# Rotary halves swapped by GpSimd's SBUF-to-SBUF transfers in place of permutation products, the sign in the sine table

## What is computed

```python
def rope(t):
    ...
    t1, t2 = tf[..., : hd // 2], tf[..., hd // 2 :]
    rot = jnp.concatenate([-t2, t1], axis=-1)
    return (tf * jnp.cos(ang) + rot * jnp.sin(ang)).astype(t.dtype)
```

```python
def partial_rope(x, cos, sin):
    half = cos.shape[-1]
    rot = 2 * half
    xr = x[..., :rot].astype(jnp.float32)
    x1, x2 = xr[..., :half], xr[..., half:]
    out = jnp.concatenate([x1 * cos - x2 * sin, x2 * cos + x1 * sin], axis=-1).astype(x.dtype)
    return jnp.concatenate([out, x[..., rot:]], axis=-1)
```

## Time and profile before

| | |
|---|---|
| median of 3 runs | 3019.54 us (3014.81 to 3020.39) |
| span of the profiled execution | 3020.7 us |
| TensorE busy | 2978.3 us, 99% |
| VectorE busy | 2178.2 us, 72% |
| ScalarE busy | 1275.6 us, 42% |
| GpSimd busy | 128.6 us, 4% |
| mean granted clock of TensorE | 0.995 |
| projection 0 | about 489 to 635 us |
| projection 1 | about 1469 to 1617 us |
| projection 2 | about 2418 to 2566 us |

### The profile page before, as it was taken

The page is one execution under the profiler, slowest core; times in us unless marked ns, Lnnn a source line. Parts: engine busy times, 40 slices in busy tenths (PEclk is TensorE's granted clock), DMA queues, the critical chain, the costliest instruction groups (busy, mean ns, idle before and its releaser), DMA issues.

```text
span 3020.7 us, 46546 instructions
## 1 busy us (share of the span) xinstructions
PE 2978.3 (99%) x17415; PEld 2601.4 (86%) x17415; DVE 2178.2 (72%) x3215; ACT 1275.6 (42%) x1903; POOL 128.6 (4%) x121
## 2 busy tenths in 40 slices
PE   8999999999999999999999999999999999999998
PEld 7888888887888889998877899988998878799987
DVE  7577765765777678785688787867775478788753
ACT  4333223465332245452345554425454244654442
POOL 0000000000000000000031000000000013000000
PEclk9999999999999999999999999999999999999999
DMA  4355553213555533343322133442333322123332
GB/s 162 99 191 194 188 196 99 84 43 95 176 181 192 191 106 103 104 148 114 92 81 63 57 105 103 155 153 84 106 108 103 101 79 84 36 91 104 105 105 76
DMA packets 263452, 351.94 MB, mean 117 GB/s; under 512 B 16770, under 2 KB 208500, under 8 KB 263312
## 3 DMA queue, kind: packets, MB, share of 16 engines
q1 hardware_dynamic: 241344, 270.57, 28.8%
q0 software_dynamic: 21488, 79.09, 8.0%
q10 hardware_dynamic: 480, 0.35, 0.0%
HBM read 348.76 MB, written 2.10 MB: 116 GB/s over the span
## 4 chain that ended last, share of the span: by engine, by line
PE 87%; DVE 9%; ACT 2%; issue 2%; DMA 0%; POOL 0%; DVEq 0%; SPq 0%; ACTq 0%
PE bank L2237 18%; PE bank L2239 18%; PE bank L2238 18%; PE bank L2378 9%; PE bank L2380 9%; PE bank L2381 9%; DVE w_lo L1324 1%; PE bank L2298 1%; PE bank L2260 1%; PE bank L2263 1%; PE bank L2261 1%; DVE a_score L1824 1%; ACT w_hi L754 0%; DVE h_f L1379 0%; DVE h_lo L1385 0%
## 5 line engine op out<-in xcount | busy, mean ns | idle before, releaser
L1324 DVE TENSOR_TENSOR w_lo<-raw,w_hi 128x1024 fp32r<-128x1024 f32 x322 | 393.8, 1224 | 510.8 <-ACT w_hi L754 508.0
L754 ACT ACTIVATE w_hi<-raw 128x1024 fp32r<-128x1024 f32 x348 | 368.6, 1059 | 894.9 <-PE bank L2239 844.8
L2237 PE MATMUL bank<-h_hi,w_hi 128*128 128x512 f32 x1376 | 541.8, 394 | 4.3 <-POOL w_lo L702 2.6
L2239 PE MATMUL bank<-h_hi,w_lo 128*128 128x512 f32 x1376 | 537.1, 390 | 0.0
L2238 PE MATMUL bank<-h_lo,w_hi 128*128 128x512 f32 x1376 | 536.5, 390 | 0.0
L2237 PE MATMUL bank<-act_hi,w_hi 128*128 (+1 forms) x1120 | 437.8, 391 | 0.0
L2239 PE MATMUL bank<-act_hi,w_lo 128*128 (+1 forms) x1120 | 436.1, 389 | 0.0
L2238 PE MATMUL bank<-act_lo,w_hi 128*128 (+1 forms) x1120 | 435.8, 389 | 0.0
L2237 PEld LDWEIGHTS bank<-h_hi,w_hi 128*128 128x128 f32 x1376 | 259.0, 188 | 61.5 <-issue 8.1
L2239 PEld LDWEIGHTS bank<-h_hi,w_lo 128*128 128x128 f32 x1376 | 258.8, 188 | 54.8
L2238 PEld LDWEIGHTS bank<-h_lo,w_hi 128*128 128x128 f32 x1376 | 259.2, 188 | 52.5
(11 more groups left out here) (382 smaller groups left out, 5695.3 us busy)
## 6 DMA issues: line engine op xcount, KB each, us to landing
raw<-in_ffn_w_in_dram SPq DMA_DIRECT2D x176, 512.0 KB, 3.5
ada_w<-in_ada_w_dram POOLq DMA_DIRECT2D x72, 1024.0 KB, 5.6
raw<-in_ffn_w_out_dram SPq DMA_DIRECT2D x88, 512.0 KB, 3.6
raw<-in_ffn_w_gate_dram SPq DMA_DIRECT2D x44, 512.0 KB, 3.8
raw<-in_ffn_w_up_dram SPq DMA_DIRECT2D x44, 512.0 KB, 3.9
raw<-in_ffn_w_down_dram SPq DMA_DIRECT2D x44, 512.0 KB, 4.3
raw<-in_mix_w_in_dram SPq DMA_DIRECT2D x44, 512.0 KB, 3.6
raw<-in_attn_w_qkv_dram SPq DMA_DIRECT2D x24, 512.0 KB, 3.7
```

Of the source, the lines that this page charges most:

```text
L754: nc.scalar.activation(w_hi[:, nb % SPL, :], raw_slab(nb), ACT.Copy).then_inc(s_hi, 1)
L1324: V.tensor_tensor(w_lo[:, nb % SPL, :], raw_slab(nb), w_hi[:, nb % SPL, :].bitcast(F32), ALU.subtract).then_inc(s_lo, 1)
L2237: T.matmul(dst, wh, mh, start=first, stop=False)
L2239: return T.matmul(dst, wl, mh, start=False, stop=last)
```

## The change

The halves are now swapped by transfers. ScalarE's copy goes to st in plain float32; GpSimd issues, for each rotated tile, four transfers that write the rows of st with the halves of each head exchanged into swap (`swap_halves`): 32 rows of 2 KB each in projection 0, 8 rows each in projections 1 and 2. Each waits for the copy of its tile, and from tile 2 on for the rotation of the tile two before. VectorE waits for the four (`s_swap`, one semaphore for each place), multiplies swap by the sines in place and adds it to rot; st_lo, turned and the two products of a tile are gone. The sign now stands in the tables: in the sine table of projection 0, and for projections 1 and 2 in the frequencies of the first half (negative angle; the cosine is the same). The rows of swap that no transfer writes in projections 1 and 2 are cleared once per layer. The sums by quarters, which VectorE made at the start, come as a constant, and `keep_warm` reads a tile of ones. TensorE's counts for the transposed tiles (`s_postmm`) are renumbered, and these use bank 4 + idx % 2.

On GpSimd, in the order of its list, the place is projection 1: the tables' loads are followed by w_lo of slabs 10 to 22 before (the ISA row is the instruction that configures GpSimd for its subtraction; ada_w is the load of the next FFN).

The diff, cut:

```diff
-    half_turn = np.zeros((P, P), np.float32)
-    part_turn = np.zeros((P, P), np.float32)
...
+    quarters = np.tile(np.eye(32, dtype=np.float32), (4, 4))
...
+    sign = np.where(np.arange(P) % HD < HD // 2, -1.0, 1.0)[:, None]
+    rope = np.concatenate([np.cos(ang), sign * np.sin(ang)], 1).astype(np.float32)
...
-        small[h:h + rot // 2, 64] = f2
+        small[h:h + rot // 2, 64] = -f2
...
+        def swap_count(m, i):
+            return 64 * (((0, 8, 14), (0, 8, 13))[i % 2][m] + i // 2 + 1)
...
+            def swap_halves(m, i):
+                rows = HD // 2 if m == 0 else HD // 8
+                pool.wait_ge(s_actT, AT0[f"proj{m}"] + i + 1)
+                if i >= 2:
+                    pool.wait_ge(s_rot, RO0[m] + i - 1)
+                for h in (0, HD):
+                    for to, src in ((h, h + rows), (h + rows, h)):
+                        pool.dma_start(side["swap"][to:to + rows, i % 2, :], side["st"][src:src + rows, i % 2, :]).then_inc(s_swap[i % 2], 16)
...
             mix_tables(0)
+            for i in range(16):
+                swap_halves(0, i)
...
             mix_tables(1)
-            project_lo(1)
+            for i in range(9):
+                swap_halves(1, i)
+            project_lo(1, (POOL_LO[0], POOL_LO[0] + 3))
+            for i in (9, 10):
+                swap_halves(1, i)
+            project_lo(1, (POOL_LO[0] + 3, POOL_LO[1]))
...
-                            nc.scalar.activation(bufs["st_hi"][:, staged % 2, :], src, ACT.Copy).then_inc(s_actT, 1)
+                            nc.scalar.activation(bufs["st"][:, staged % 2, :], src, ACT.Copy).then_inc(s_actT, 1)
...
+                if step == 4:
+                    link(V.memset(side["swap"][:], 0.0))
...
-                        dve.wait_ge(s_postmm, PO0[m] + j + 1)
-                        if i:
-                            dve.wait_ge(s_rot, RO0[m] + i)
-                        link(V.tensor_tensor(bufs["turned"][:], aux[:], bufs["cos"][:, 1, :], ALU.mult))
-                        V.tensor_tensor(rot, rot, bufs["turned"][:], ALU.add).then_inc(s_rot, 1)
+                        swap = bufs["swap"][:, i % 2, :]
+                        dve.wait_ge(s_swap[i % 2], swap_count(m, i))
+                        link(V.tensor_tensor(swap, swap, bufs["cos"][:, 1, :], ALU.mult))
+                        V.tensor_tensor(rot, rot, swap, ALU.add).then_inc(s_rot, 1)
...
-                        V.tensor_tensor(bufs["st_lo"][:, j % 2, :], src, bufs["st_hi"][:, j % 2, :].bitcast(F32), ALU.subtract)
...
-            V.tensor_copy(turn_hi[:], squares[:, 1:3, :]).then_inc(s_ones, 1)
...
-                            T.matmul(aux[:], turn, bufs["st_hi"][:, j % 2, :], start=True, stop=False)
-                            pe.wait_ge(s_dveT2, RO0[m] + rotated[0] + 1)
-                            ins = T.matmul(aux[:], turn, bufs["st_lo"][:, j % 2, :], start=False, stop=True)
```

90 lines of the change are left out of this document (41 added, 49 removed).

## The result

The changed kernel takes 3039.4 us (median of 4 runs, 3036.8 to 3040.8) and the kernel before, run beside it, 3018.6 us (4 runs, 3014.8 to 3020.4): the ratio is 1.0068, with a 95% interval of 1.0055 to 1.008. The forecast was 3038 us. The profiled execution of the changed kernel spans 3035.0 us against 3020.7 before.

The account below looks back on a forecast made before the run. TensorE, busy 99% of the span, was taken as the bound, with VectorE and GpSimd close in the projections. Projection 0's -4.1 plus 2 x (7 + 3 + 1) gives +17.9 on 3019.5: 3037.4, taken as 3038 us; range 3024 to 3055.

Parts of the forecast that it names:

- part 2: Projections 1 and 2: w_lo queued behind transfers, TensorE waits 8.8 us (slab 10), 3.6 (slab 13); less products, +7 a layer.
- the 1515 that was announced: Sign: TensorE waits 8 to 10 us for GpSimd's w_lo near 1515 and 2480, then products 0.43 us apart.
- part 4: Projections 1 and 2: VectorE work reading two SBUF operands collides with GpSimd's w_lo; 1 us a layer, bounds 0 and 3.6.
- part 3: Projections 1 and 2: products behind TensorE's waits run at half clock; 3 us a layer, bounds 0 and 5.2.
- part 1: All projections: 76 turning products go, 17.2 us of TensorE's time: 7.3 in the first, 5.0 in each other.
- part 5: Projection 0: products' saving less waits for VectorE's low parts and transfer landings; -4.1 us, bounds -4.4 and +4.
- the step from 6.2 to 7: Projections 1 and 2: one layer without clock sums to +6.2 us, carried group by group +7.7; 7 was taken.
- A program brought in on GpSimd: Rival: ahead of slab 10's w_lo in projection 1, GpSimd's first subtraction loads a program, 6 us, total 3044; chance 0.14.
- Slow transfers in projection 0: Rival: landing above 5 us or issues of 0.8 us turn projection 0's -4.1 into +4, total 3046; chance 0.10.
- The queue in time: Rival: GpSimd reaches w_lo of slab 10 in time, only the gains remain, total 3005; chance 0.08.
- No change: Rival: waits overlap with slack further on, only some 5 us a layer remain without a clock drop, 3020; chance 0.06.

Follow-up runs that it names:

- experiment 2: Changed kernel with each transfer split into two column halves: in projections 1 and 2, time grew by 27 us; in projection 0 alone, 21 us above the changed kernel.
- experiment 1: Changed kernel with GpSimd's list reordered in projections 1 and 2: w_lo of slabs 10 and 13 ahead of transfers, 3029.1 us; w_lo and tiles alternating, 3022.4 us.
- no_transfers_p12: Changed kernel without the transfers of projections 1 and 2 and VectorE's wait for them, rotation there not computed: 3014.4 us.

## Why the prediction was right, step by step

**GpSimd's queue (part 2): right in mechanism and nearly in size.** Waits of 8.49 and 4.61 us stood where 8.8 and 3.6 were forecast, in both layers. The first began at 1522.1 us in projection 1, some 7 us later in the span than the 1515 that was announced; that number followed from no sum. The parts: eight issues took 3.98 us for 4.3 assumed, because one holds GpSimd 0.50 us and not 0.54; w_lo 2.4. The second wait is 1 us longer than forecast because of the held score sum, a collision of the kind that part 4 counts. Doubling the issues (experiment 2) and reordering them (experiment 1) both move the waits as the queue says.

**The clock (part 3): right in kind, a little low.** 3 us a layer were taken. Keeping TensorE busy brings back 3.0 and 3.1 us, or 6.7 us by the medians for both; by the products behind the waits the clock cost 4.0 and 4.2 us. The 3.4 us of half speed, which part 3 sets as its lower end, stand in none of the rows shown with the prediction; the trace of before has one such stretch, at 1466 to 1469 us.

**The products (part 1): counted in full, which held only beside the long waits.** 5.0 us a layer were counted as gained. The changed kernel's projections agree with it (13.1 us of waits, less 1.3 that stood there before, less 5.0, plus 4.1 for the clock is 10.9; measured 10.9 and 10.9), because TensorE's long waits leave every later chain in time. Without the waits just 1.5 and 1.7 us come through (no_transfers_p12). The view that would have shown this is VectorE's timeline before slab 13, not TensorE's busy share.

**VectorE against GpSimd (part 4): right, and the main term next.** 1 us a layer was taken. The score sum held beside w_lo of slab 12 (2.50 us for 0.75) makes the wait before slab 13 about 1 us longer than the queue alone was forecast to. The other collision fell into time that TensorE waits anyway: tile 9's multiply took 4.32 us in projection 1 and TensorE was not late for it. In the mended orders such collisions are what is left. The Trainium skill, "SBUF — State Buffer", section "Who interferes with whom", says that a VectorE instruction with two SBUF inputs contends with a GpSimd instruction that reads SBUF. The runs agree, with their own sizes: 0.75 us became 2.50 and 2.89, 0.69 us became 4.37 and 4.75, and moving three w_lo to VectorE brought 0.75 back.

**Projection 0 (part 5): right in sign, its inner assumptions wrong both ways.** -4.1 was forecast; the profile has -5.5, of which 2.7 are the clock of before, so -2.8. The landing was taken as 3.6 us and is 1.9 there, so the transfers hide; TensorE waits 4.2 us for VectorE's w_lo (1.36, 1.33, 0.60 and 0.88) where four waits of 0.9 were forecast. Of the 7.3 us of products 3.2 go into these waits (1.0 us stood there before) and 2.8 come through; where the other 1.3 went was not traced. That they hide is not a wide margin: experiment 2 turned 4 us more of issues per pair into some 21 us.

**The total: partly luck.** The forecast had -4.1 and twice 11 (7 for the queue less the products, 3 for the clock, 1 for the collisions), +17.9 us. Measured behind the openings are -2.8 and twice 10.9, +19.0 us, and 20.8 us between the medians. The 10.9 are about 5.8 for the queue less the products, 4.1 for the clock and 1.0 for the collision: the step from 6.2 to 7 (part 2) and the clock (part 3) erred by about 1 us each, in opposite directions. That 3038 met 3039.4 within 2 us is closer than the parts.

**The rivals.** A program brought in on GpSimd (the time would have been 3044): w_lo of slab 10 starts at 1528.23, 0.09 us after the last issue, and the first wait is no longer in projection 1 (8.49 us) than in projection 2 (8.41), so nothing was loaded there. The Trainium skill, "GPSIMD Engine Reference", section "2.1 Instruction dispatch", has about 6 us for the first call of a freshly loaded kernel; no row here shows it. Slow transfers in projection 0: not here, as the landing shows. The queue in time (3005): refuted by the waits. No change: refuted.

**What one profile can't tell.** Stretches of half clock outside the edited stages differ from trace to trace, and "between" in the table of stages runs from -3.8 to +3.2 us. The openings show how much of this falls inside the stages too, up to 2.7 us in one. A profile of one execution can't settle a question of 3 us unless such stretches are set apart, and the medians of eight to eleven runs still leave intervals of 3 us to either side.
